# Last stage of a mixture-of-experts block: weight loads and splits moved inside the last expert, matmul passes regrouped

## The reference

```
x = x + moe_ffn(rms_norm(x, moe_norm), ...)            # 32 experts, each w_up 1024x2048, w_down 1024x1024
h = rms_norm(x, ple_norm)
x = x + sigmoid(h @ ple_gate_w) * (p @ ple_proj_w)     # ple_gate_w 1024x1024, ple_proj_w 256x1024
out = rms_norm(x, final_norm)
```

## Time and profile before

| | us |
|---|---|
| median of 3 runs | 1220.18 |
| lowest and highest | 1218.33, 1222.06 |
| the profiled execution, its own time | 1222.13 |
| its span, first to last instruction | 1220.0 |
| PE busy in the span | 1167.0 (96%), mean granted clock 0.985 |
| DVE, ACT, POOL busy | 445.6, 234.9, 99.7 |
| moved by DMA | 447.00 MB, 366 GB/s over the span |

### The profile page before, as it was taken

How to read it: one execution, slowest core, us unless ns; L and a number is a source line. 1 busy time by engine, 2 the same in 40 slices (tenths; PEclk the granted TensorE clock), 3 DMA queues, 4 the chain that set the end, 5 groups by cost and what they waited for, 6 DMA issues and landing times.

```text
span 1220.0 us, 15132 instructions
## 1 busy us (share of the span) xinstructions
PE 1167.0 (96%) x5958; PEld 539.1 (44%) x5958; DVE 445.6 (37%) x683; ACT 234.9 (19%) x309; POOL 99.7 (8%) x52
## 2 busy tenths in 40 slices
PE   6988999999999999999999999999999999999986
PEld 5988999733333333333333333333333333333335
DVE  4899987432222222222222222222222222222243
ACT  4332573311111111111111111111111111111152
POOL 4082424100000000000000000000000000000020
PEclk8989999999999999999999999999999999999988
DMA  7754545989999999999999999999999999999930
GB/s 242 247 208 132 173 150 220 407 370 391 423 428 429 429 428 428 428 428 429 430 428 428 427 430 428 429 429 428 381 422 428 429 429 428 429 429 428 423 147 35
DMA packets 58424, 447.00 MB, mean 366 GB/s; under 512 B 4099, under 2 KB 26875, under 8 KB 33819
## 3 DMA queue, kind: packets, MB, share of 16 engines
q1 hardware_dynamic: 57291, 443.68, 87.8%
q0 software_dynamic: 672, 1.99, 0.6%
q10 hardware_dynamic: 432, 0.92, 0.2%
HBM read 445.52 MB, written 1.05 MB: 366 GB/s over the span
## 4 chain that ended last, share of the span: by engine, by line
PE 75%; DMA 9%; DVE 6%; issue 5%; ACT 4%; DVEq 1%; SPq 0%; ACTq 0%
PE ps L1442 32%; PE ps L1489 18%; DMA down_ring<-in_expert_w_down_dram 8%; PE ps L1503 5%; PE ps L1399 4%; PE ps L1450 4%; DVE xs L946 3%; PE ps L1279 3%; ACT picked L774 3%; PE ps L1343 2%; PE ps L1355 2%; PE ps L1408 2%; PE ps L1563 1%; DMA down_ring<-in_conv_w_dram 1%; PE ps L1511 1%
## 5 line engine op out<-in xcount | busy, mean ns | idle before, releaser
L1442 PE MATMUL ps<-up_ring,hT 128*64 128x512 f32 x2048 | 446.6, 594 | 0.9 <-issue 0.9
L1442 PEld LDWEIGHTS ps<-up_ring,hT 128*64 128x64 f32 x2048 | 147.8, 137 | 293.8 <-issue 293.8
L1489 PE MATMUL ps<-down_ring,hT 128*64 128x512 f32 x1024 | 233.8, 598 | 3.3 <-DMA down_ring<-in_expert_w_down_dram 2.7
L1138 DVE TENSOR_SCALAR work<-ps 128x512 f32<-128x512 f32 x32 | 22.1, 692 | 536.9 <-PE ps L1450 536.9
L1489 PEld LDWEIGHTS ps<-down_ring,hT 128*64 128x64 f32 x1024 | 68.6, 136 | 143.4 <-issue 134.8
L1156 DVE TENSOR_TENSOR x_sb<-x_sb,ps 128x1024 f32<-128x1024 f32 x66 | 80.1, 1214 | 141.2 <-PE ps L1503 135.8
L786 ACT ACTIVATE work<-work 128x512 f32<-128x512 f32 x32 | 20.2, 630 | 484.2 <-DVE work L1138 484.2
L1279 PE MATMUL ps<-h_hi,w_hi 128*128 128x256 f32 x320 | 83.5, 296 | 14.6 <-DVE w_lo L415 7.0
L420 POOL TENSOR_TENSOR w_lo<-up_ring,g_hi 128x2048 fp32r<-128x2048 f32 x2 | 9.1, 4529 | 957.8 <-ACT g_hi L817 957.8
L1279 PE MATMUL ps<-h_hi,w_lo 128*128 128x256 f32 x320 | 82.2, 292 | 0.0
L675 ACT ACTIVATE w_hi<-up_ring 128x2048 fp32r<-128x2048 f32 x32 | 61.3, 1915 | 106.0 <-PE ps L1279 66.3
(11 more groups left out here) (232 smaller groups left out, 931.2 us busy)
## 6 DMA issues: line engine op xcount, KB each, us to landing
up_ring<-in_expert_w_up_dram SPq DMA_DIRECT2D x128, 2048.0 KB, 21.7
down_ring<-in_expert_w_down_dram SPq DMA_DIRECT2D x64, 2048.0 KB, 15.5
up_ring<-in_w_in_dram SPq DMA_DIRECT2D x22, 1024.0 KB, 5.1
up_ring<-in_branch_w_dram SPq DMA_DIRECT2D x6, 1024.0 KB, 5.0
up_ring<-in_w_out_dram SPq DMA_DIRECT2D x4, 1024.0 KB, 4.9
up_ring<-in_ple_gate_w_dram SPq DMA_DIRECT2D x4, 1024.0 KB, 22.4
x_sb<-in_x_dram SPq DMA_DIRECT2D x1, 1024.0 KB, 5.1
up_ring<-in_ple_proj_w_dram SPq DMA_DIRECT2D x1, 1024.0 KB, 17.2
```

What stands on the lines that cost most here:

```text
L1442: last = nc.tensor.matmul(ps[64 * g:64 * g + 64, GLU + part, :], xe[:, j, k % 4, k // 4, :], w[:, D * part + 512 * g:D * part + 512 * (g + ...
L1489: last = nc.tensor.matmul(ps[64 * g:64 * g + 64, Y, :], actT[:, r, c, :], down_units[:, c, D * r + 512 * g:D * r + 512 * (g + 1)], start=( ...
```

## The change

- **SP:** the five transfers for the last stage (`load_ple`) are issued after the up transfers of expert 31 and before its two down transfers. The flag is read earlier.
- **ACT and DVE:** expert 31 has its own copy of the code, in which ACT makes `g_hi` quarters 0 and 1 after the copy of `actT`, quarter 2 after that of `weightT` and quarter 3 after that of `y_sb`; DVE makes `w_lo` quarters 0 and 1 around its second addition for expert 30, and quarters 2 and 3 later. POOL makes none now.
- **PE, result of expert 31:** the second 128 tokens' result goes to PSUM banks 4 and 5 directly behind the first (no wait for DVE between them). Projections move behind them, and the two for the first 128 tokens behind the first gate passes.
- **PE, gate product:** for the first 128 tokens all high x high matmuls, then all with low activations, then all with low weights. For the other 128 tokens the columns go as 512, 256 and 256, so there are five pieces and not four.
- **ACT:** the sums of squares of x come behind the scaled high part; the table of the sigmoid is loaded by a dummy activation before the first sigmoid, and the table of the square root by another behind the last sigmoid. The partial sums are added with the scale and the bias of the next small activation, one for each of the five pieces.

```diff
+FINAL = [(0, 0, 512), (0, 512, 512), (1, 0, 512), (1, 512, 256), (1, 768, 256)]
+FINAL_BANK = [4, 5, 1, 2, 4]
+PROJ_BANK = [3, 0, 6, 7]
...
+            q = N_EXP - 2
+            refill_up(q, 0, q)
+            refill_down(q, q)
+            refill_up(q + 1, 1, q + 1)
...
+            with sp.If(overflow < 1):
+                sp.wait_ge(w_used, used_before(N_EXP - 2) + UP_UNITS)
+                load_ple()
+                refill_down(q + 1, q + 1)
...
-            for m in (1, 2):
-                pool.wait_ge(g_hi_ready, m + 1)
-                gate_lo_part(nc.gpsimd, m).then_inc(g_lo_ready[m], 1)
...
                 nc.scalar.activation(actT[:, :, :, :].rearrange("p m g s -> p (m g s)"), ps[:, ACTT, :],
                                      ACT.Copy).then_inc(actT_ready, 1)
+                if with_gate:
+                    split_gate(0)
+                    split_gate(1)
...
-            root().then_inc(rms_ready, 1)
+            own(root())
+            nc.scalar.activation(small[:, 34:35], eps, ACT.Sigmoid).then_inc(rms_ready, 1)
             act.wait_ge(rstd_ready, 2)
...
+            nc.scalar.activation(small[:, 34:35], eps, ACT.Sqrt)
+            for i, (a, at, n) in enumerate(FINAL):
+                act.wait_ge(ple_x_ready, i + 1)
+                own(nc.scalar.activation(xs[:, a, at:at + n], x_sb[:, a, at:at + n], ACT.Square,
+                                         accum_out=part_ssq[:, i:i + 1]))
+                last = at + n == D
+                before_it = eps if at == 0 else mean_sq[:, i - 1 - a:i - a]
+                out_it = rms[:, a:a + 1] if last else mean_sq[:, i - a:i - a + 1]
+                ins = nc.scalar.activation(out_it, part_ssq[:, i:i + 1], ACT.Sqrt if last else ACT.Identity,
+                                           bias=before_it, scale=1.0 / D)
...
                 add_result(q - 1, 0)
                 scale_xe(q + 1, 1 - j)
+                if with_gate:
+                    split_gate(0)
                 add_result(q - 1, 1)
+                if with_gate:
+                    split_gate(1)
...
             def finish(q):
 
 
-                pe.wait_ge(ple_proj_loaded, 16)
                 pe.wait_ge(weightT_ready, q + 1)
-                ple_projection(0, 0)
                 pe.wait_ge(y_ready, q + 1)
                 to_tokens(q, 0)
-                ple_projection(0, 1)
-                pe.wait_ge(x_final, 1)
                 for g in range(2):
-                    last = nc.tensor.matmul(ps[:, COMB + g, :], weightT[64 * g:64 * g + 64, 1, :],
+                    last = nc.tensor.matmul(ps[:, WT + g, :], weightT[64 * g:64 * g + 64, 1, :],
                                             y_sb[64 * g:64 * g + 64, :], start=True, stop=True)
                 last.then_inc(comb_done, 1)
+                pe.wait_ge(x_final, 1)
                 transpose_tokens(x_sb, 0, 0)
+                pe.wait_ge(ple_proj_loaded, 16)
+                ple_projection(1, 0)
                 pe.wait_ge(x_final, 2)
                 transpose_tokens(x_sb, 1, 0).then_inc(xsT_done, 1)
...
-            pe.wait_ge(flag_ready, 1)
-            overflow = pe.value_load(flag[0:1, 0:1], min_val=0, max_val=1)
             with pe.If(overflow > 0):
...
+            for w, h in ((g_hi, h_hi), (g_hi, h_lo), (w_lo, h_hi)):
+                for k in range(KT):
...
+                    for i in range(2):
+                        last = gate(i, w, h, k)
...
             for h in range(2):
+                ple_projection(0, h, done=h)
+            for i in range(2, len(FINAL)):
...
+                for k in range(KT):
+                    for w, h in ((g_hi, h_hi), (g_hi, h_lo), (w_lo, h_hi)):
+                        last = gate(i, w, h, k)
+                last.then_inc(ple_gate_done, 1)
```

More of the change, by code:

```diff
@@ L173, in build @@
         most = small[:, 32:33]
-        half_ssq = small[:, 36:40]
+        part_ssq = small[:, 42:47]
+        mean_sq = small[:, 47:50]
         frstd = small[:, 40:42]
@@ L507, in _ @@
                     refill_down(2 * i + j - 1, 2 * i + j - 1)
+            sp.wait_ge(flag_ready, 1)
+            overflow = sp.value_load(flag[0:1, 0:1], min_val=0, max_val=1)
             q = 2 * AHEAD_PAIRS
@@ L780, in _, with split_gate, expert @@
             nc.scalar.activation(gateT, ps[0:N_EXP, WT, 0:T], ACT.Copy).then_inc(gateT_ready, 1)
-            def expert(q):
+            def split_gate(m):
+                act.wait_ge(ple_gate_loaded[m], 16)
+                nc.scalar.activation(g_hi[:, m, :], up_ring[:, m, :], ACT.Copy).then_inc(g_hi_ready, 1)
+            def expert(q, with_gate=False):
                 act.wait_ge(glu_ready, q + 1)
@@ L812, in _ @@
                         expert(2 * i + j)
[L814 to L821, removed]
+                for m in range(4):
+                    split_gate(m)
+            act.wait_ge(x_final, 1)
+            act.dma_start(final_gain, on_all(final_norm)).then_inc(gain_loaded, 16)
+            act.wait_ge(xsT_done, 3)
@@ new lines, in _ @@
+            for i, (a, at, n) in enumerate(FINAL):
+                act.wait_ge(ple_x_ready, i + 1)
[6 more added lines that the diff above has]
+                                           bias=before_it, scale=1.0 / D)
+                if last:
+                    ins.then_inc(final_rms, 1)
+                else:
+                    own(ins)
@@ L1182, in _ @@
                 last_results(ROUNDS * N_EXP - 1)
-            with dve.If(overflow < 1):
-                last_results(N_EXP - 1)
+                for m in range(2):
+                    split_gate(m)
+            split_gate(2)
             scale_low(3, 0, ROW["ple_norm"], h_hi)
@@ L1533, in _ @@
                 expert(q, q, 0, first=q == 0)
+            pe.wait_ge(flag_ready, 1)
+            overflow = pe.value_load(flag[0:1, 0:1], min_val=0, max_val=1)
             with pe.Fori(1, N_EXP // 2) as i:
@@ new lines, in _, with gate @@
+            ple_projection(1, 1)
+            hT_written(3)
+            def gate(i, w, h, k):
+                a, at, n = FINAL[i]
+                m, row = divmod(k, 2)
+                return nc.tensor.matmul(ps[:, FINAL_BANK[i], at % 512:at % 512 + n],
+                                        h[:, k, a * P:(a + 1) * P], w[:, m, D * row + at:D * row + at + n],
+                                        start=(k == 0 and w is g_hi and h is h_hi), stop=(k == KT - 1 and w is w_lo))
+            for w, h in ((g_hi, h_hi), (g_hi, h_lo), (w_lo, h_hi)):
+                for k in range(KT):
+                    if h is h_hi and w is g_hi and k % 2 == 0:
+                        pe.wait_ge(g_hi_ready, k // 2 + 1)
+                    if h is h_lo and k % 4 == 0:
+                        pe.wait_ge(h_lo_ready, 3 + k // 4)
+                    if w is w_lo and k % 2 == 0:
+                        pe.wait_ge(g_lo_ready[k // 2], 1)
+                    for i in range(2):
+                        last = gate(i, w, h, k)
+                        if w is w_lo and k == KT - 1:
+                            last.then_inc(ple_gate_done, 1)
```

126 lines of the change are left out of this document (57 added, 69 removed).

## The result

The changed kernel takes **1223.33 us** (median of 10 runs, 1221.21 to 1225.21) against 1220.53 (10 runs) for the kernel before in the same session: 2.8 us more, ratio 1.0023 with a 95% interval of 1.0014 to 1.0032. That is inside 0.3%, and inside the range of the prediction, but 2.1 us above the +0.7 us of its sum, and 2.4 us above its 1220.9. Its profiled execution took 1222.9 us, with a span of 1220.4 us.

The account below looks back on a forecast made before the run. PE bounds the kernel, busy 1167.0 of 1220.0 us; +4.3 wait, +1.7 clock, −1.2 gap, −8.6 up to the gates, +3.8 gates, +0.7 tail make +0.7 us, forecast 1220.9 us. Range for 8 in 10: 1217.0 to 1224.5.

Parts of the forecast that it names:

- its sum: Whole span against 1220.0 us: all gains and losses of the change together, +0.7 us.
- The transfers: SP's queue: last-stage weights down at 1160.2, expert 31's down parts at 1165.1 and 1170.0.
- rival 3: SP's queue stalls on held issues, second down part lands late; at 5 us more 1225.9; chance 0.10.
- rival 1: Expert 31's down parts aren't late, so all 6.0 us of delay are won: 1214.9; chance 0.10.
- The wait: PE idle at expert 31's first down part from 1160.81 to 1165.1: 4.3 us lost.
- The clock: PE at half speed for 3.4 us after its idle time at the first down part: 1.7 us lost.
- rival 2: A second fall of PE's clock behind the 1.1 us gap, another 1.7 us: 1222.6; chance 0.25.
- The gap: PE idle behind expert 31's second down part, set by its sequencer's branch: 1.1 us instead of 2.29.
- From the gap to the end: Behind expert 31's result: gates start at 1184.3 and last 25.6 us, tail 10.8 us.
- The splits: Gate weight splits on DVE, 2.28 us each with POOL quiet, fit around other work: cost 0.
- the flag's load: On PE's sequencer, moved to the start of the experts: cost 0, 0.9 us at most.
- 1.95 above the median: Excess of the kernel before's profiled execution (1222.13 us) over its runs' median, 1220.18, taken off the forecast.

Follow-up runs that it names:

- after: The changed kernel as first measured and profiled, nothing further altered: 1223.33 us, ratio 1.0023 to the kernel before.
- again: The changed kernel, unchanged, run once more for a second profile: 1222.88 us, ratio 1.0021 to the kernel before.
- passes_back: The changed kernel with the gate passes of the first 128 tokens put back in their old order: 1222.42 us, ratio 1.0019 to the kernel before.
- early_squares: The changed kernel with ACT's sums of squares moved between the sigmoids: 1219.16 us, ratio 0.9991 to the kernel before.
- order_alone: The kernel before with only SP's transfers moved, last stage's weights ahead of expert 31's down transfers: 1228.81 us, ratio 1.0074.
- near_branch: The changed kernel with SP's old transfer order and PE's last-stage code right behind the expert loop: 1217.00 us, ratio 0.9965 to the kernel before.
- before_again: The kernel before, unchanged, run once more for a second profile: 1221.41 us, ratio 1.0004.
- warm: The changed kernel with 36 unread identity transposes on PE ahead of the wait for expert 31's down weights: 1222.53 us.
- experiment 2: The changed kernel with only SP's order undone, expert 31's down transfers first again: 1218.71 us, ratio 0.9982 to the kernel before.
- experiment 1: Both kernels run once more, unchanged, for second profiles: changed kernel 1222.88 us, kernel before 1221.41 us.
- experiment 7: near_branch with ACT's split of gate quarter 2 moved behind its copy of y_sb: 1215.83 us, ratio 0.9963 to the kernel before.

## Why the prediction was right, and where its sum was short

**The transfers: right.** The down transfers landed at 1165.0 and 1169.8 (predicted 1165.1 and 1170.0), the last gate quarter at 1135.7 + 24.4 = 1160.1 by SP's row for L536 (predicted 1160.2). SP was held as feared: the first down issue came at 1144.6, far ahead of the 1160.2 from which rival 3 would have counted, and the queue didn't run dry. Rival 3 is out, and rival 1 too, since all four profiles that carry both the order and the other parts (after, again, passes_back, early_squares) show the wait, and so does order_alone.

**The wait: 4.3 us by the sum, 5.4, 4.6, 5.4 and 5.1 in those four profiles.** I had set the landing against 1160.81, the time at which PE reaches the down parts in one execution of the kernel before. In the changed kernel's PE got there at 1159.64. This arrival differs by up to 3.7 us between profiles of kernels that are the same up to there (near_branch 1157.88, before_again 1161.56), and the landing mostly moves along (after 1165.0, again 1163.3). Why it differs is open. That the second part ended at 1175.12 (predicted 1175.1) is thus partly luck: PE came 1.2 us earlier and waited 1.1 us longer. Between arrival and landing there are 0.9 us more on the mean of the four than I took. The step that was short can be named: the down part landed 17.6 or 17.7 us behind the last up part of expert 31 in all four, as summed; but that up part landed only 12.2 to 13.0 us ahead of PE's arrival, where both profiles of the kernel before have 13.3. Why it landed later is open too.

**The clock: right.** The first part took 5.38 us, predicted 3.58 + 1.7; PE worked at half speed from 1165.07 to 1168.6, 3.5 us where I had taken 3.4. The warm variant shows it to be the clock. No second fall came behind the gap (rival 2): the clock was 1.00 from 1169 on, and the transposes took 1.04 us.

**The gap: 0.74 us, predicted 1.1**, and not as I had it. The branch took 3.72 us and not 4.51, so it ended ahead of the copy of `y_sb`, which I had named as the low end. The runs show that it is the jump that is dear (0.07 us for the fall-through), and that DMA traffic makes it dearer. Of thirteen far branches, one in each profile, the four that began while weights were still landing took 4.51, 4.93, 5.83 and 5.99 us, the nine that began after the traffic 3.34 to 3.77. In each of them the trace has one packet of 16 KiB on a DMA queue of the kind `instruction`, and the branch ends 1.4 us after this packet does. Without traffic the packet starts 1.0 us after the branch; in the four with traffic it starts after 2.0, 2.4, 3.4 and 3.5 us. Here it is in the stretch 1169.1 to 1170.3 of experiment 2 (branch from 1165.7), and in 1172.6 to 1174.1 of the changed kernel (branch from 1171.7); in the 3.5 us of the branch before the first of these stretches there is none (queue, kind: packets, MB, share of 16 engines):

```profile
q8 instruction: 1, 0.02, 5.6%
```

```profile
q8 instruction: 1, 0.02, 5.5%
```

The Trainium skill, Runtime: NRT & Kernel Launch, section Instruction fetch mechanics, says that a taken branch to a target outside the pages held waits for a DMA fetch of that page, and these traces agree. By that reading the sum would have been 0.5 us lower, and this step nearer, though the whole further off.

**From the gap to the end: right.** Gates started at 1183.76 (predicted 1184.3), lasted 25.8 us (25.6), and the tail took 10.8 (10.8). The splits cost nothing: 2.28 to 2.29 us each on DVE, since POOL was out of it. Moving the flag's load cost nothing that shows: PE's matmuls follow each other without idle time where it now stands (306.8 us).

**So the span of the profiled execution met the sum** (1220.0 + 0.7 = 1220.7, measured 1220.4), partly by luck as said, and it is the step to the median that failed, with three parts.

- *The execution summed against.* I took "1.95 above the median" off the sum, as if the excess of the profiled execution would be there in the changed kernel too. But 1.3 us of it may be the low clock of its last stage, which experiment 1 does not show, and the change replaces just this stage.
- *The wait* is 0.9 us longer on the mean, as said above.
- *Outside the span.* I took the time outside the span, 2.13 us, as unchanged and so put it at nothing. Over all runs it is 2.0 us for the kernel before and for order_alone, and 2.3 to 2.5 for every kernel that has the new code of PE, ACT and DVE: 0.4 us of the difference, from a cause that no run shows.

With all three the sum is 0.7 + 1.3 + 0.9 + 0.4 = 3.3 us; the medians say 2.8, with 1.7 to 3.9 as the interval. If the usual execution of the kernel before lies between its two profiles, it is some 0.6 us less. None of the parts is measured to better than half a microsecond. The stages say the same. From PE's arrival to the end of the second down part it is 8.2 us in both profiles of the kernel before and 14.5 to 15.5 in the four of the changed order. From there to the end of the span it is 51.0 and 49.7 us before, and 45.3 in both profiles of the changed kernel, where the sum had 45.6.

**Where the expected gain went.** 6.0 us of delay at the down parts were bought for an earlier arrival of weights that had no taker: with the old order of transfers (experiment 2) the gates start at 1181.0 all the same, because what stood in their way was the split on DVE, the wait between the two halves of the result, and the projections. (Once the branch is near, one quarter of the weights does come late, but moving its split back cures that without moving a transfer, experiment 7.) Those the change did remove, and they are worth 1.5 us by medians even with the 2.9 us gap behind the far branch. The move of the transfers took 4.2 us, and the whole came out as a loss.

## What to carry to other kernels

When a queue is never empty, moving a transfer ahead makes every one behind it later by its whole length: compare that length (here 12.7 us) with the slack of what is passed (8 us), and ask who would start earlier. When a sum is made from one profiled execution, take a second one of the same kernel before trusting the stage that the change replaces; its clock there may be a part of the gain. Look at the sequencer's branches and at small steps that queue up in front of an idle engine's last work: here a jump made near and squares moved into idle time were worth more than all the loads.

## What the runs showed of the hardware

- A branch over the repeated loop cost PE's sequencer 3.34 to 3.77 us without DMA traffic (nine profiles), 4.51 to 5.99 us while weights were landing (four), and 0.07 us when it fell through; on ACT the branch took 0.05 us. A 16 KiB packet of the kind `instruction` starts 1.0 us after the far branch without traffic and 2.0 to 3.5 us after it with, and the branch ends 1.4 us behind the packet.
- A split of 128x2048 on DVE took 2.28 us alone, and 5.09 us with POOL doing the same on another quarter beside it for 4.3 us, while POOL's own took 4.54 and 5.79.
- Four issues of 1 MiB held SP for 19.35 us, while expert 31's up transfers were in flight, and the transfers still landed in the order of issue, with 4.9 us for each 2 MiB.
- A square runs between two sigmoids on ACT without a table load; a square root takes one (1.28 us).
